# The norm's factor moved from the gate/up results into the token operands, with three plain groups first

## The reference

```python
def rmsnorm(x, g):
    y = xf * lax.rsqrt(jnp.mean(xf * xf, axis=-1, keepdims=True) + EPS)
    return (y * g.astype(jnp.float32)).astype(x.dtype)

def swiglu_half(x, g_pre, w_gate, w_up, w_down, g_post):
    h = rmsnorm(x, g_pre)
    y = (jax.nn.silu(h @ w_gate) * (h @ w_up)) @ w_down
    return x + 0.5 * rmsnorm(y, g_post)
```

## Time and profile before

| | us |
|---|---|
| median of 3 runs | 1672.21 (1671.72 to 1672.41) |
| profiled execution: its time / its span | 1679.09 / 1677.3 |
| busy, share of the span: TensorE / VectorE / ScalarE / GpSimd | 89% / 54% / 37% / 26% |
| one seven-product group to the next, first half step (mean of 18) | 14.34 |
| factor's end to first down product, first half step | 311.4 |
| the same, second half step | 305.9 |

### The profile page before, as it was taken

How to read it: one execution, slowest core, us unless ns; L and a number is a source line. 1 busy time by engine, 2 the same in 40 slices (tenths; PEclk the granted TensorE clock), 3 DMA queues, 4 the chain that set the end, 5 groups by cost and what they waited for, 6 DMA issues and landing times. The chain is left out here.

```text
span 1677.3 us, 31039 instructions
## 1 busy us (share of the span) xinstructions
PE 1498.0 (89%) x12072; PEld 1364.9 (81%) x12072; DVE 900.5 (54%) x1393; ACT 615.8 (37%) x1070; POOL 438.6 (26%) x407
## 2 busy tenths in 40 slices
PE   6777878789999999999998999989978888787997
PEld 6777877789988888887876877789977878787996
DVE  5766666622264767334476533464576666664124
ACT  6344443422252245321134233343653343433222
POOL 2444555400026000223201220110045445552000
PEclk9889899999999999999999999989998899999999
DMA  4122222232267987999997577644412222213322
GB/s 156 51 76 76 76 75 66 71 138 87 93 211 248 356 311 262 354 333 330 372 349 252 175 248 260 234 170 147 137 53 69 71 76 76 76 64 121 105 86 69
DMA packets 114848, 275.76 MB, mean 164 GB/s; under 512 B 15721, under 2 KB 18410, under 8 KB 113698
## 3 DMA queue, kind: packets, MB, share of 16 engines
q1 hardware_dynamic: 108050, 249.66, 43.3%
q0 software_dynamic: 6240, 23.28, 3.9%
q10 hardware_dynamic: 432, 1.05, 0.2%
HBM read 257.55 MB, written 16.39 MB: 163 GB/s over the span
## 5 line engine op out<-in xcount | busy, mean ns | idle before, releaser
L212 ACT ACTIVATE w_high<-w_raw 128x1024 fp32r<-128x1024 f32 (+1 forms) x93 | 107.9, 1161 | 460.4 <-PE psum L237 410.3
L216 DVE TENSOR_TENSOR w_low<-w_raw,w_high 128x1024 fp32r<-128x1024 f32 (+1 forms) x93 | 125.9, 1354 | 243.9 <-ACT w_high L212 242.8
L1149 PE MATMUL psum<-sums_high,gu_high 128*128 128x260 f32 x480 | 152.4, 317 | 108.7 <-DVE halves L1000 60.1
L1149 PE MATMUL psum<-h_high,gu_high 128*128 128x260 f32 x640 | 191.2, 299 | 15.5 <-DVE silu L944 12.7
L1149 PEld LDWEIGHTS psum<-sums_high,gu_high 128*128 128x128 f32 x480 | 101.4, 211 | 122.5 <-DVE halves L1000 67.3
L1150 PE MATMUL psum<-h_low,gu_high 128*128 128x260 f32 x640 | 189.9, 297 | 0.0
L1151 PE MATMUL psum<-h_high,gu_low 128*128 128x260 f32 x640 | 188.3, 294 | 0.0
L1151 PE MATMUL psum<-sums_high,gu_low 128*128 128x260 f32 x480 | 148.3, 309 | 0.0
L1149 PEld LDWEIGHTS psum<-h_high,gu_high 128*128 128x128 f32 x640 | 131.1, 205 | 16.9 <-DVE silu L944 13.0
L233 PE MATMUL psum<-mix_h_high,w_high 128*128 128x260 f32 x672 | 139.9, 290 | 1.1 <-issue 1.1
L235 PE MATMUL psum<-mix_h_low,w_high 128*128 128x260 f32 x672 | 136.2, 284 | 0.8 <-issue 0.8
(11 more groups left out here) (439 smaller groups left out, 3584.5 us busy)
## 6 DMA issues: line engine op xcount, KB each, us to landing
kv_ring<-in_cache_k SPq DMA_DIRECT2D x256, 256.0 KB
kv_ring<-in_cache_v SPq DMA_DIRECT2D x256, 256.0 KB
w_raw<-in_w_dn SPq DMA_DIRECT2D x32, 704.0 KB
w_raw<-in_w_proj SPq DMA_DIRECT2D x44, 512.0 KB
raw_even<-in_w_gu SPq DMA_DIRECT2D x40, 512.0 KB, 3.5
raw_odd<-in_w_gu SPq DMA_DIRECT2D x40, 512.0 KB, 3.4
spill<-h_f POOLq DMA_DIRECT2D x20, 260.0 KB
gates<-spill POOLq DMA_DIRECT2D x16, 260.0 KB, 4.3
```

Source lines behind the costliest of these rows:

```text
L212: act.activation(w_high[:, u, 0:nk, :], w_raw[:, u, 0:nk, :], ACT.Copy).then_inc(high_done, 1)
L216: dve.tensor_tensor(w_low[:, u, 0:nk, :], w_raw[:, u, 0:nk, :], w_high[:, u, 0:nk, :].bitcast(F32), ALU.subtract).then_inc(low_done, 1)
L1149: pe.matmul(out, wh[:, slot, :], hi, start=start, stop=False, skip_group_check=True)
```

## The change

1. **The factor goes into the tokens.** The tokens `xw` (now `x_normed`) carry the factor: even chunks are rebuilt on GpSimd as `h_high + h_low` (step add) and multiplied by the factor, odd ones come from one VectorE instruction each. `h_high`/`h_low` are rewritten from them (steps token) once the plain groups are done, and t0 to t3 are sums of them. GpSimd's four products per group, g1f, c22f, g2f and late1, are gone; S3 and S4 stay there. SiLU reads VectorE's results without GpSimd between them.
2. **A third plain group.** G0 is 3: group 2 is computed plainly (its 96 matmuls stand in for 84), which gives the tokens time; 19 groups per half step remain in the seven-product form in place of 20. The plain groups still get the factor on their results (scale, and late on GpSimd).
3. **New orders** on TensorE, VectorE, ScalarE and GpSimd, and new PSUM banks.

```diff
-G0 = 2
+G0 = 3
...
 
 def unit_order():
 
-    order = [("gate", 1), ("up", 1)]
-    for n in range(G0, KF + 1):
-        for kind, m in (("PA", n), ("P7", n - 1), ("P5", n), ("P6", n), ("P4", n - 1), ("P3", n - 1)):
-            if G0 <= m < KF:
-                order.append((kind, m))
+    order = [("gate", 1), ("up", 1), ("gate", 2), ("up", 2), ("P5", G0), ("PA", G0), ("P6", G0), ("P7", G0)]
+    for n in range(G0 + 1, KF):
+        order += [("PA", n), ("P3", n - 1), ("P5", n), ("P6", n), ("P4", n - 1), ("P7", n)]
+    order += [("P3", KF - 1), ("P4", KF - 1)]
     return order
...
-def pool_steps():
...
-    for n in range(G0, KF):
-        s += [t for t in (("g2f", n - 2), ("S3", n), ("S4", n), ("g1f", n), ("c22f", n - 1), ("late1", n))
-              if G0 <= t[1] < KF and (n > G0 or t[0] not in ("S3", "S4"))]
...
+        s += [t for t in (("g1", n), ("hid2", n - 2), ("c12", n - 1), ("P7", n), ("PA", n + 1), ("S1", n + 1),
+                          ("S2", n + 1), ("P3", n), ("low", n - 2), ("P5", n + 1),
+                          ("hid1", n - 1), ("P6", n + 1), ("P4", n), ("c22", n)) if G0 <= t[1] < KF]
+    return s + [("hid2", KF - 2), ("down", 0), ("c12", KF - 1), ("low", KF - 2), ("hid1", KF - 1), ("hid2", KF - 1),
...
+POOL_STEPS = [("add", k) for k in range(0, KD, 2)] + [("xw", k) for k in range(0, KD, 2)] + [
+    ("t", 0), ("late", 0), ("t", 1), ("late", 1), ("t", 2), ("t", 3), ("late", 2)] + [(t, n) for n in range(G0, KF) for t in ("S3", "S4")]
+ACT_STEPS, DVE_STEPS = act_steps(), dve_steps()
...
-                    load(G0 + 1, 1)
-                    for n in range(G0 + 2, KF):
+                    sp.wait_ge(gu_pool, G("xw", KD - 2))
+                    sp.wait_ge(gu_dve, V("xw", KD - 1))
+                    load(3, 0)
+                    load(3, 1)
+                    sp.wait_ge(gu_dve, V("second", 3))
+                    load(4, 0)
+                    load(4, 1)
+                    for n in range(5, KF):
                         sp.wait_ge(gu_pool, G("S4", n - 2))
                         load(n, 0)
                         sp.wait_ge(gu_dve, V("P4", n - 2))
...
                     load_block(sp, w_dn, 0, nb, 0, NKD)
...
+                    def normed(k):
+
+                        pool.wait_ge(gu_pool, G("add", k))
+                        pool.tensor_tensor(xw[:, k, :], xw[:, k, :], factor[:, :], ALU.mult).then_inc(gu_pool, 1)
+
+                    for k in range(0, KD, 2):
+                        pool.wait_ge(h_low_done, m0 + k + 1)
+                        pool.tensor_tensor(xw[:, k, :], h_high[:, k, :].bitcast(F32), h_low[:, k, :].bitcast(F32),
+                                           ALU.add).then_inc(gu_pool, 1)
+                    pool.wait_ge(norm_rec, norm_n + 1)
+                    for k in range(0, KD, 2):
+                        normed(k)
+                    pool.wait_ge(gu_pool, G("xw", KD - 2))
+                    pool.tensor_tensor(t1[:, :, :], xe1, xe2, ALU.subtract).then_inc(gu_pool, 1)
+                    late(0)
+                    pool.wait_ge(gu_dve, V("xw", KD - 1))
+                    pool.wait_ge(gu_pool, G("t", 0))
+                    pool.tensor_tensor(t2[:, :, :], xo2, t1[:, :, :], ALU.add).then_inc(gu_pool, 1)
+                    late(1)
+                    pool.wait_ge(gu_pool, G("t", 1))
+                    pool.tensor_tensor(t4[:, :, :], xo1, t2[:, :, :], ALU.subtract).then_inc(gu_pool, 1)
+                    pool.tensor_tensor(xe2, xo2, xe2, ALU.subtract).then_inc(gu_pool, 1)
...
-                    def gate_first_late(n):
-                        pool.wait_ge(gu_act, A("silu1", n))
-                        pool.tensor_tensor(g1[n % 2], g1[n % 2], fac1, ALU.mult).then_inc(gu_pool, 1)
...
-                    pool.tensor_tensor(t2[:, :, :], xo2, xe1, ALU.add).then_inc(gu_pool, 1)
-                    late(0)
-                    pool.wait_ge(norm_rec, norm_n + 1)
-                    sum_three(G0)
...
+                        sum_three(n)
+                        sum_four(n)
...
                     def gate_first_silu(n):
-                        act.wait_ge(gu_pool, G("g1f", n))
+                        act.wait_ge(gu_dve, V("g1", n))
                         act.activation(g1[n % 2], g1[n % 2], ACT.Silu).then_inc(gu_act, 1)
 
                     def gate_second_silu(n):
-                        act.wait_ge(gu_pool, G("g2f", n))
+                        act.wait_ge(gu_dve, V("c12", n))
                         act.activation(g2, g2, ACT.Silu).then_inc(gu_act, 1)
...
 
                         dve.wait_ge(gu_act, A("second", u))
-                        dve.tensor_tensor(c_low[:, u, :, :], c_raw[:, u, :, :], c_high[:, u, :, :].bitcast(F32),
+                        src = c_raw[:, u, :, :] if u < 2 else raws[0][:, u - 2, :, :]
+                        dve.tensor_tensor(c_low[u // 2][:, u % 2, :, :], src, c_high[u // 2][:, u % 2, :, :].bitcast(F32),
+                                          ALU.subtract).then_inc(gu_dve, 1)
+
+                    def normed(k):
+
+                        dve.scalar_tensor_tensor(out=xw[:, k, :], in0=x[:, k, :], scalar=vecs[:, v_pre + k:v_pre + k + 1],
+                                                 in1=factor[:, :], op0=ALU.mult, op1=ALU.mult).then_inc(gu_dve, 1)
+
+                    def token_low(k):
+
+                        dve.wait_ge(gu_act, A("token", k))
+                        tok = slice(0, T if k % 2 else HT)
+                        dve.tensor_tensor(h_low[:, k, tok], xw[:, k, tok], h_high[:, k, tok].bitcast(F32),
...
                         dve.wait_ge(gu_used, at("P4", n))
-                        dve.wait_ge(gu_pool, G("late1", n))
+                        dve.wait_ge(gu_act, A("silu1", n))
                         if n > G0:
...
+                    unit_low("PA", G0)
+                    sum_two(G0)
+                    unit_low("P5", G0)
+                    unit_low("P6", G0)
+                    gate_scale(2)
+                    dve.wait_ge(gu_act, A("t", 2))
+                    dve.tensor_tensor(t_lo[:, 8:10, :], t4[:, 0:2, :], t_hi[:, 8:10, :].bitcast(F32), ALU.subtract)
...
+                    for k in range(KD):
+                        token_low(k)
+                    sum_low(3, T3_LOW, xe2, T3_HIGH)
+                    hidden(2)
+                    low(2)
                     for n in range(G0, KF):
                         gate_first(n)
                         if n >= G0 + 2:
                             hidden_second(n - 2)
-                        if n < LAST:
-                            sum_one(n + 1)
                         if n > G0:
-                            up_second(n - 1)
-                            unit_low("P3", n - 1)
+                            gate_second(n - 1)
+                        unit_low("P7", n)
                         if n < LAST:
                             unit_low("PA", n + 1)
...
-                        if n < LAST:
-                            unit_low("P5", n + 1)
+                            sum_one(n + 1)
+                            sum_two(n + 1)
+                        unit_low("P3", n)
                         if n >= G0 + 2:
                             hidden_low(n - 2)
                         if n < LAST:
-                            sum_two(n + 1)
+                            unit_low("P5", n + 1)
                         if n > G0:
                             hidden_first(n - 1)
                         if n < LAST:
                             unit_low("P6", n + 1)
-                        if n > G0:
-                            gate_second(n - 1)
                         unit_low("P4", n)
-                    up_second(LAST)
-                    unit_low("P3", LAST)
...
+                    pe.wait_ge(gu_dve, V("scale", 0))
+                    second_products(2)
+                    pe.wait_ge(gu_dve, V("hid", 0))
+                    second_products(3)
...
                             else:
-                                pe.wait_ge(gu_dve, V("scale", 1) if n == G0 else V("hid", 1))
+                                pe.wait_ge(gu_dve, V("scale", 2) if n == G0 else V("hid", 2))
                             for j in range(4):
+                                if n == G0:
+                                    pe.wait_ge(gu_dve, V("token", 2 * j + 1))```

The order changes at three places. **First, VectorE inside the seven-product stage**, one whole group (`gu_low` is a unit's low part: from `sums_gate` P7 or P3, from `sums_up` P5 or P6, from a raw tile 128x1024 PA, 128x512 P4; L995 is g1, L1021 hid2, L973 S1, L982 S2, L1000 c22, L1007 c12, L1014 hid1, L1025 low). Before, from g1 of a group to S2 of the next:

```order
L995 TENSOR_TENSOR halves_61<-psum,halves_61 128x260
L1021 TENSOR_TENSOR hidden_half_66<-halves_61 128x260
L973 TENSOR_TENSOR sums_up_64<-raw_odd_58 128x512
L1000 TENSOR_TENSOR halves_61<-psum,halves_61 128x260
L990 TENSOR_TENSOR gu_low_60<-sums_gate_65,gu_high_59 128x512
```

(30 more changed lines are left out.)

210 lines of the change are left out of this document (97 added, 113 removed).

## The result

The changed kernel takes 1518.34 us (median of 4 runs, 1517.62 to 1520.0); before, on the same chip, 1672.31 (4 runs, 1671.72 to 1672.51). The ratio is 0.9081, 95% interval 0.9065 to 0.9097. The forecast was 1534.6 in a range of 1508 to 1578; 1518.34 lies at the lower edge of its likeliest case (1518 to 1556). The profiled execution took 1520.0 with a span of 1518.0.

What follows compares the result with a forecast made beforehand. A loop through up's transfer was taken to bound the group at 14.3 us. Factor to first down product, 38.5 + 18 x 10.5 + 8.5 = 236.0, with the adds' delay saves 138.2: 1672.21 becomes 1534.6, range 1508 to 1578.

Steps and rivals of the forecast that it cites:

- likeliest case: Whole kernel: 10.2 to 10.9 us per seven-product group, 1518 to 1556 us in all; chance 0.60.
- What bounds the kernel: Seven-product stage before: a loop from P4 through up's load, S1 and back to P4, 3.4 + 10.9 = 14.3 us a group.
- The group after the change: Seven-product group, new order: 10.5 us, bounds 10.05 and 11.7, with the clock at 1.00; 14.34 before.
- the loop 7.1 + 3.4: Seven-product group after: 7.1 us from up's landing through S1 to P4, plus 3.4 for the transfer: 10.5.
- my second sum: VectorE's work per group after: 7.7 us of its own plus about 1.2 for each of S3 and S4: 10.1.
- The first rival: Seven-product stage at TensorE's rate, 10.05 us a group, the start's turns mostly hidden: about 1515 us; chance 0.12.
- The turns: GpSimd and VectorE instructions with two SBUF inputs alternate; S3 and S4 each hold VectorE about 1.2 us a group.
- the rival that the factor was hidden: Seven-product stage: removing the factor's products gives nothing, the period stays at 14.3 us; within a chance of 0.04.
- The adds ahead of the factor: Start of each half step: GpSimd's four adds delay the factor by 4.1 us in the first, 3.0 in the second.
- Factor to g1 of group 3: Start of a half step: 38.5 us, from the sum of GpSimd's and VectorE's turns and later steps; 37.6 before.
- The end of a half step: Last g1 to first down product: 8.5 us after the change, 15.6 before.
- The rival with a stall near 2 us and the half clock in each group: Seven-product stage: stall for c22 or g1 remains, period up to 12.2 us, 1596 us in all; chance 0.15.

Runs made afterwards that it cites:

- even_on_scalar: Changed kernel without GpSimd's four adds ahead of the factor; ScalarE makes the four even token tiles behind it: 1519.71 us, ratio 0.9035 to the kernel before.
- products_back_after: Changed kernel with GpSimd's four products per group put back in the new order, the factor applied twice: 1571.15 us, ratio 0.9344 to the kernel before.
- no_products_before: Kernel before without GpSimd's four products per group, old order kept, factor missing from its results: 1629.92 us, ratio 0.9697.

## Why the prediction was right, and where it was off

**What bounds the kernel: right.** Halving the load took from the group what it took from the landing (0.9 and 0.9 us), so the loop through the transfer was the period of before.

**The group after the change: right in size, and not by the loop alone.** I took 10.5 us from the loop 7.1 + 3.4; it is 10.3. But S1 waits for its load in 7 of 14 groups and never over 0.3 us, and half loads gain 0.07. What stands beside the loop is my second sum, VectorE's 10.1: 134.38/140 x 10.34 = 9.9 busy, and the period is still 10.27 when the load is short. From S1 at 173.55 to the end of P4's low part at 180.40 the loop takes 6.85 us, where I had 7.1; with a transfer of 3.4 to 3.5, through which VectorE works on, that is 10.3 to 10.4. Loop and VectorE's sum have become nearly one length, and shortening the loop wins the 0.07 alone. The first rival, TensorE's rate, would have it at 10.05; that shows once the turns are short (10.08). Whether the loop would have stood at 10.27 or lower without VectorE in the way, the runs don't tell.

**The turns: right.** Two turns cost 2.0 us a group, for which I had 2.4; a third costs 1.12. The Trainium skill, "GPSIMD Engine Reference" (section 1, Specifications), names the contention with instructions of two SBUF inputs; by that rule the trace agrees (1.78 us in place of 0.68 beside S4), and the page has no price for it.

**The share of the products: not asked for.** The prediction took products and order together, and held the SiLU's wait for GpSimd (83 us) against the rival that the factor was hidden. Asked one by one, the products were worth 1.1 to 1.2 us a group and the orders 2.8, so that rival was nearer than its price said. My expectations of 1587 and 1605 put the products at 2.3 and at 2.4 us or more a group: a wait of up to 5.7 us on ScalarE was worth 1.1 us to the loop.

**The adds ahead of the factor:** +3.2 and +2.5 for the +4.1 and +3.0 of the sum. Three of VectorE's rows grew by 1.0 to 1.1 where they met an add, and the first, an instruction of L329, by 0.6 (1.33 for 0.76), where the sum had four of about 1.2; with the adds gone (`even_on_scalar`) 2.4 to 2.7 and 2.9 us come back.

**Factor to g1 of group 3:** 39.8 us for 38.5; a sum of turns again, since work moved from GpSimd to VectorE gains 1.7 only.

**The end of a half step:** 8.2 us for 8.5.

**The step that failed: the down products.** The forecast held, but its sum ends at the first down product and takes what follows as unchanged. It isn't, by -4.75 and -5.82 us, and without this the miss would have been 4 us in place of 14.5. The issue of the load of x and of the down blocks behind it waits for `low` of the last group. Before, SyncE's queue came to it 344.40 - 336.95 = 7.5 us behind the first down product; now it is 266.69 - 262.40 = 4.3. Of these 3.2 us, 1.2 come from the last g2, which ends 1.4 us behind that product before and 0.2 after; 0.8 from GpSimd's last product (L724) between g2 and its SiLU; and 1.2 from the steps from the SiLU to `low`, where VectorE now does the last hid2 ahead of a down block's low part of 1.6 us and not behind it. From the second profiles, for before and then for after, the issue of the load of x and the first product of the third down block, which waited for that queue:

```profile
344.40 0.33 SPq L675 DMA_DIRECT2D x<-in_x  x1
```

```profile
358.27 0.80 PE L233 MATMUL psum<-a_high,w_high 128*128 128x260 f32 x2 [3.71 <-DVE w_low L216]
```

```profile
266.69 0.33 SPq L664 DMA_DIRECT2D x<-in_x  x1
```

```profile
280.35 0.50 PE L222 MATMUL psum<-a_high,w_high 128*128 128x260 f32 x2 [1.84 <-DVE w_low L205]
```

The idle fell by 1.9 us, and the clock's fall behind it is gone in this stretch. The windows of ten microseconds in which the product lies, before and after:

```profile
357.00:367.00 10.00, 8.72 (x61) 8.73 (x62) 2.83 (x2) 2.16 (x3) 0.00 (x0) 0.83 0.43 146
```

```profile
272.00:282.00 10.00, 8.15 (x68) 7.95 (x67) 3.23 (x2) 3.75 (x4) 0.00 (x0) 1.00 0.56 215
```

TensorE is busy for 8.72 us there and starts 61 matmuls, where at 0.12 us each it would start 73: the fall cost about 1.4 us (an estimate from this row). The rest of the first half step's 4.75 us has nothing to do with the load. These are the ten microseconds from the first down product on, before and after:

```profile
337.00:347.00 10.00, 10.00 (x71) 10.00 (x72) 3.97 (x7) 3.61 (x4) 0.74 (x1) 0.83 0.18 40
```

```profile
262.00:272.00 10.00, 9.95 (x83) 9.77 (x83) 4.33 (x8) 3.50 (x4) 0.00 (x0) 1.00 0.44 156
```

Before, the clock is at its lower level at the start of them, behind the wait of 2.15 us ahead of the first down product that the earlier trace rows shows and that is gone after: 71 matmuls in place of 83, again about 1.4 us. In the second half step the clock at that point is 1.00 in both kernels; there the idle of the third block falls from 4.72 to 1.51 us, and the ten microseconds behind it hold 61 matmuls at a clock of 0.70 before and 85 at 1.00 after.

That the earlier load is the cause of the shorter idle rests on these rows; no run moved the load by itself. With the term in it, the sum would have been -149 us and the forecast 1524.

**The clock.** The rival with a stall near 2 us and the half clock in each group did not come. The Trainium skill, "TensorE: Matmul & The Clock Gate" (HAM oscillation), describes such a pattern for waits of about 3 to 5 us on a transfer, after each of which the next tile starts at the lower clock. In this case the falls of the kernel before stand behind shorter idles (1.91 us, for L1000, ahead of the half microseconds at 0.50 from 240 us on), so by these rows a stall near 2 us was enough. Without such a stall the clock stays up: `products_back_after` has an idle of up to 1.0 us for g1 in nearly every group at a clock of 1.00, while `no_products_before`, with one of up to 2.1 us, is at 0.96.

## What to carry to other kernels

When two engines take turns, sum their work as if they were one and compare it with every loop that goes through a transfer; over the group that sum was good to 0.2 us, over the start moved onto VectorE it was not (27 us for 38.1). Taking work off the engine behind the longest wait brings less than the wait says until another order opens that loop (here 1.1 us a group against 2.8). And follow a change past the end of its stage: what the last instruction of the stage releases (here a load of 2 MB and the blocks queued behind it) starts earlier too, and belongs in the sum.

## What the hardware did that I had not expected

The mixer, whose code no kernel here touches, takes 690.1 to 691.5 us in the profiles from some chips and 696.9 to 698.0 from others, within 1.1 us for the kernels that shared a chip, before and after alike. The 199 us behind its factor, in after on two chips:

```profile
422.00:621.00 199.00, 199.00 (x1905) 170.97 (x1904) 119.30 (x184) 70.91 (x98) 41.85 (x44) 1.00 0.90 313
```

```profile
421.00:620.00 199.00, 195.11 (x1845) 166.97 (x1847) 117.65 (x182) 68.14 (x93) 38.65 (x41) 0.99 0.86 298
```

One moved 313 GB/s and had TensorE busy throughout, the other 298 and left it idle for 4 us. The difference of 7 us in a profile of before from one chip and of after from another looked like a gain of the change, and was none. Why the chips differ stays open.
